# A four-layer transformer kernel: new head tiles copied before the output scale, the log forget gate turned onto 128 partitions, the convolution's norm one row step later

## The reference

```python
# differential attention, 8 heads; q, k: two maps of 64 each, v: 128
p = softmax(mask(q @ k.T * scale - slope_h * distance))      # per map
a = p[0] - lam * p[1]
o = rmsnorm(a @ v, g_sub) * (1 - lambda_init)

# odd mixer: forgetting attention (8 heads of 64) beside a conformer convolution
log_f = log_sigmoid(p[..., 1536:1544] + forget_b)            # (512, 8)
cum = cumsum(log_f, axis=positions)
logits[t, s] = q_t . k_s / 8 + cum[t] - cum[s]               # causal
y_c = softmax(logits) @ v
h = a * sigmoid(b)                                           # 512 channels
h = causal_dwconv(h, 31 taps) + dw_b
y_d = silu(layer_norm(h over channels) * cn_g + cn_b)
out = concat(y_c, y_d) @ w_out
```

## Time and profile before

| | us |
|---|---|
| median of 3 runs | 2386.34 (2384.98 to 2386.59) |
| the profiled execution | 2386.98 |
| its span | 2385.2 |
| PE busy in the span | 2304.6 (97%) |
| DVE, ACT, POOL busy | 722.7, 706.6, 1036.3 |
| granted TensorE clock, mean | 0.987 |

### The profile page before, as it was taken

How to read it: one execution, slowest core, us unless ns; L and a number is a source line. 1 busy time by engine, 2 the same in 40 slices (tenths; PEclk the granted TensorE clock), 3 DMA queues, 4 the chain that set the end, 5 groups by cost and what they waited for, 6 DMA issues and landing times.

```text
span 2385.2 us, 24593 instructions
## 1 busy us (share of the span) xinstructions
PE 2304.6 (97%) x10287; PEld 1847.2 (77%) x10287; DVE 722.7 (30%) x1361; ACT 706.6 (30%) x992; POOL 1036.3 (43%) x358
## 2 busy tenths in 40 slices
PE   8999999999999989999999999999998998999998
PEld 6667888887677768888878878888876666888887
DVE  6535000004566350000057310000169635000003
ACT  2453221222333232212222232222252563221221
POOL 3124554553333245545445555545432224554543
PEclk9999999999999999999999999999999999999999
DMA  4113323221211132322222323222320112323221
GB/s 166 72 71 124 106 89 106 88 85 69 112 54 54 53 106 88 106 89 97 97 92 92 105 106 100 94 97 88 102 75 29 56 58 80 132 88 106 89 88 53
DMA packets 32222, 212.60 MB, mean 89 GB/s; under 512 B 3568, under 2 KB 4720, under 8 KB 9072
## 3 DMA queue, kind: packets, MB, share of 16 engines
q1 hardware_dynamic: 32112, 211.03, 25.6%
HBM read 208.92 MB, written 2.10 MB: 88 GB/s over the span
## 4 chain that ended last, share of the span: by engine, by line
PE 89%; DVE 8%; ACT 2%; issue 1%; POOL 0%; DMA 0%; DVEq 0%; SPq 0%
PE bank L894 17%; PE bank L896 17%; PE bank L895 17%; PE bank L944 9%; PE bank L946 9%; PE bank L945 9%; PE bank L925 3%; DVE bank L1894 2%; PE bank L1004 2%; PE bank L930 1%; PE bank L1077 1%; PE bank L1324 1%; PE bank L982 1%; DVE X L1577 1%; PE bank L1245 1%
## 5 line engine op out<-in xcount | busy, mean ns | idle before, releaser
L754 POOL TENSOR_TENSOR wlo<-raw,whi 128x2048 fp32r<-128x2048 f32 (+4 forms) x183 | 842.1, 4604 | 664.4 <-ACT whi L432 664.4
L894 PE MATMUL bank<-XH,whi 128*128 128x512 f32 x1824 | 720.5, 395 | 9.6 <-POOL wlo L808 6.3
L896 PE MATMUL bank<-XH,wlo 128*128 128x512 f32 x1824 | 712.4, 391 | 0.0
L895 PE MATMUL bank<-XL,whi 128*128 128x512 f32 x1824 | 712.1, 390 | 0.0
L432 ACT CAST whi<-raw 128x2048 fp32r<-128x2048 f32 (+4 forms) x183 | 348.4, 1907 | 392.5 <-PE bank L944 304.5
L894 PEld LDWEIGHTS bank<-XH,whi 128*128 128x128 f32 x1824 | 343.9, 189 | 97.1 <-issue 18.6
L896 PEld LDWEIGHTS bank<-XH,wlo 128*128 128x128 f32 x1824 | 343.8, 188 | 72.8
L895 PEld LDWEIGHTS bank<-XL,whi 128*128 128x128 f32 x1824 | 344.2, 189 | 69.1
L1600 DVE TENSOR_TENSOR hf<-sil,bank 128x512 f32<-128x512 f32 x88 | 60.5, 688 | 902.9 <-PE bank L896 855.1
L768 POOL TENSOR_TENSOR HL<-hf,HH 128x512 fp32r<-128x512 f32 x88 | 114.0, 1295 | 400.2 <-ACT HH L470 400.2
L944 PE MATMUL bank<-whi,HH 128*128 128x512 f32 x704 | 274.4, 390 | 0.0
(11 more groups left out here) (258 smaller groups left out, 2120.9 us busy)
## 6 DMA issues: line engine op xcount, KB each, us to landing
raw<-w_ffn_gu SPq DMA_DIRECT2D x88, 1024.0 KB, 4.8
raw<-w_ffn_dn SPq DMA_DIRECT2D x40, 1024.0 KB, 4.8
raw<-w_diff_in SPq DMA_DIRECT2D x7, 1536.0 KB, 6.7
GB<-gb SPq DMA_DIRECT2D x8, 1024.0 KB, 6.9
raw<-w_ev_in SPq DMA_DIRECT2D x6, 1024.0 KB, 4.9
raw<-w_od_in SPq DMA_DIRECT2D x4, 1536.0 KB, 6.3
raw<-w_mla_pair SPq DMA_DIRECT2D x4, 1088.0 KB, 5.5
raw<-w_mla_o SPq DMA_DIRECT2D x4, 1024.0 KB, 5.9
```

The costliest lines, as they stand in the source:

```text
L754: pool.tensor_tensor(wlo[:, off:off + size], raw[:, off:off + size], whi[:, off:off + size].bitcast(F32), ALU.subtract).then_inc(lo_ready, 1)
L894: release(pe.matmul(out, whi[:, off:off + P], xh, start=start, stop=False))
L895: pe.matmul(out, whi[:, off:off + P], xl, start=False, stop=False)
L896: return pe.matmul(out, wlo[:, off:off + P], xh, start=False, stop=stop)
```

## The change

- Differential heads: in step j = 3 DVE copies the new k tile first and runs `scale_head` after it.
- The forget logits are written to `lfx` (8 by 512), four small matmuls on PE turn them into 32 columns of bank 3 on 128 partitions, the chain runs on tiles of 128 by 32, and four matmuls turn the result back to 8 by 512 in bank 3, from which the scan reads. The first four stand between the two tiles of the second gate pair, the last four between taps 7 and 8 of PE's convolution. ACT's Abs waits for the turned tile.
- DVE's taps: 24, 20, three times 6, and up to 6 in each row step, in place of 28, 28, three times 7, and up to 4.
- Rows, statistics, norm and columns of the convolution come one row step later; silu moves from step 11 to step 12, behind the weight split of that step.
- In the last pair `odd_out(0)` moves to the front of step 12, `odd_out(1)` to its end, and `odd_out(2)` to the end of step 15.

```diff
-        lfz, lfa, lfe, lfu, lfl, lfd, lfi, lfr = (sb(f"lf{n}", [8, S], F32, lf_stack) for n in "zaeuldir")
+        lfx, lf0 = (sb(f"lf{n}", [8, S], F32, lf_stack) for n in "x0")
+        lfz, lfa, lfe, lfu, lfl, lfd, lfi, lfr = (sb(f"lf{n}", [P, 8 * NB], F32, lf_stack) for n in "zaeuldir")
...
-            act.wait_ge(tile_free, tiles.at())
+            act.wait_ge(small_dve, 2)
             act.activation(lfa[:], lfz[:], ACT.Abs).then_inc(small_act, 1)
...
-                if s in (6, 7):
-                    keep_rows((1, 3)[s - 6])
-                if s in (9, 10):
-                    keep_cols((0, 2)[s - 9])
+                if s in (7, 8):
+                    keep_rows((1, 3)[s - 7])
+                if s in (10, 11):
+                    keep_cols((0, 2)[s - 10])
...
-                if s == 8:
+                if s == 9:
                     act.wait_ge(cn_ready, 1)
...
-                if s == 11:
+                if s == 12:
+                    split_w()
                     act.wait_ge(cols_kept, 4)
...
-                if qb == 1 and p < 3 or s in (12, 14):
+                if qb == 1 and p < 3 or s == 14:
                     split_w()
...
-            unit_into(GLU_BANKS[1])
+            forget = tiles.n
+            off = begin_unit()
+            tile(GLU_BANKS[1][0], [off + 2 * k * P for k in range(KD)])
+            pe.wait_ge(tile_free, forget)
+            claim(3)
+            for t in range(NB):
+                ins = pe.matmul(bank[3][:, 8 * t:8 * t + 8], lfx[:, t * P:(t + 1) * P], ident[0:8, 0:8], start=True, stop=True)
+            ins.then_inc(lt_done, 1)
+            tile(GLU_BANKS[1][1], [off + (2 * k + 1) * P for k in range(KD)])
...
-            conv_taps(range(0, 16))
+            conv_taps(range(0, 8))
+            pe.wait_ge(ls_ready, 1)
+            for t in range(NB):
+                ins = pe.matmul(bank[3][0:8, t * P:(t + 1) * P], lfz[:, 8 * t:8 * t + 8], ident, start=True, stop=True)
+            ins.then_inc(lt_done, 1)
+            conv_taps(range(8, 16))
...
-                elif qb:
-                    odd_out((1, 5, 7)[qb - 1])
+                elif qb != 1:
+                    odd_out((0, None, 5, 7)[qb])
...
-                if p == 3 and qb < 3:
-                    odd_out((0, 4, 6)[qb])
+                if p == 3:
+                    odd_out((1, 4, 6, 2)[qb])
...
-            odd_out(2)
             odd_attend(3)
...
-                    if j == 3:
-                        scale_head(h - 1)
                 for t in finished(DIFF_SLOTS[2 * j] + DIFF_SLOTS[2 * j + 1], (KD,) * 3) if h < 7 else ():
                     copy_tile((dVT, dQ[1 - h % 2], dK[1 - h % 2])[t][:], t)
+                if h and j == 3:
+                    scale_head(h - 1)
...
-            take(lambda: dve.tensor_scalar(lfz[:], bank[2][0:8, :], parm[0:8, PCOL["f_b"]:PCOL["f_b"] + 1], None, ALU.add))
+            take(lambda: dve.tensor_scalar(lfx[:], bank[2][0:8, :], parm[0:8, PCOL["f_b"]:PCOL["f_b"] + 1], None, ALU.add))
+            link(dve.memset(lf0[:], 0.0))
+            dve.wait_ge(lt_done, 1)
+            dve.tensor_copy(lfz[:], bank[3][:, 0:8 * NB]).then_inc(small_dve, 1)
...
+            dve.tensor_tensor(lfz[:], lfz[:], lfr[:], ALU.subtract).then_inc(ls_ready, 1)
+            dve.wait_ge(lt_done, 2)
+            dve.tensor_tensor_scan(cum[:], bank[3][0:8, :], lf0[:], 0.0, ALU.add, ALU.add).then_inc(cum_ready, 1)
 
             glu(1)
-            taps(28)
+            taps(24)
             glu(2)
-            taps(28)
+            taps(20)
             glu(3)
...
             for t in range(3):
-                taps(7)
+                taps(6)
...
-                taps(min(4, len(taps_left)))
-                if s == 6:
+                taps(min(6, len(taps_left)))
+                if s == 7:
                     row_stats(0)
-                if s == 7:
+                if s == 8:
                     row_stats(1)
                     row_stats(2)
-                if s == 8:
+                if s == 9:
                     row_stats(3)
```

More of the change, by code:

```diff
@@ L365, in build @@
         cum_ready = sem("cum_ready")
+        lt_done = sem("lt_done")
+        ls_ready = sem("ls_ready")
         mem_ready = sem("mem_ready")
@@ L642, in _ @@
             act.activation(lfe[:], lfa[:], ACT.Exp, scale=-1.0).then_inc(small_act, 1)
-            act.wait_ge(small_dve, 2)
+            act.wait_ge(small_dve, 3)
             act.activation(lfl[:], lfu[:], ACT.Ln).then_inc(small_act, 1)
@@ L708, in _ @@
                     odd_high(p - 1)
-                if s in (6, 7):
-                    keep_rows((1, 3)[s - 6])
-                if s in (9, 10):
-                    keep_cols((0, 2)[s - 9])
+                if s in (7, 8):
+                    keep_rows((1, 3)[s - 7])
+                if s in (10, 11):
+                    keep_cols((0, 2)[s - 10])
                 for m in range(2) if s else ():
                     keep_p(fPT[m], 6 + m, (s - 1) % 4)
-                if s == 5:
+                if s == 6:
                     keep_conv(3, conv_done, 3)
-                if s in (5, 6):
-                    keep_rows((0, 2)[s - 5])
-                if s == 8:
+                if s in (6, 7):
+                    keep_rows((0, 2)[s - 6])
+                if s == 9:
                     act.wait_ge(cn_ready, 1)
@@ L723, in _ @@
                                        scale=root[:, t:t + 1]).then_inc(rows_scaled, 1)
-                if s in (9, 10):
-                    keep_cols((1, 3)[s - 9])
-                if s == 11:
+                if s in (10, 11):
+                    keep_cols((1, 3)[s - 10])
+                if s == 12:
+                    split_w()
                     act.wait_ge(cols_kept, 4)
@@ L1465, in _ @@
                         head_steps(off, ODD_SLOTS[7])
-                elif qb:
-                    odd_out((1, 5, 7)[qb - 1])
[L1468 to L1471, removed]
+                elif qb != 1:
+                    odd_out((0, None, 5, 7)[qb])
+                if s in (7, 8):
+                    rows_of((1, 3)[s - 7])
+                if s in (10, 11):
+                    cols_of((0, 2)[s - 10])
                 for m in range(2) if s else ():
@@ L1477, in _ @@
                     off = begin_unit()
-                if p == 3 and qb < 3:
-                    odd_out((0, 4, 6)[qb])
[L1480 to L1483, removed]
+                if p == 3:
+                    odd_out((1, 4, 6, 2)[qb])
+                if s in (6, 7):
+                    rows_of((0, 2)[s - 6])
+                if s in (10, 11):
+                    cols_of((1, 3)[s - 10])
             los.add(4)
@@ L1906, in _ @@
             dve.tensor_scalar(lfu[:], lfe[:], 1.0, None, ALU.add).then_inc(small_dve, 1)
-            dve.wait_ge(small_dve, 2)
+            dve.wait_ge(small_dve, 3)
             link(dve.tensor_scalar(lfd[:], lfu[:], 1.0, None, ALU.subtract))
@@ L1919, in _ @@
             link(dve.tensor_scalar(lfz[:], lfz[:], 0.0, None, ALU.min))
-            link(dve.tensor_tensor(lfz[:], lfz[:], lfr[:], ALU.subtract))
-            link(dve.memset(lfd[:], 0.0))
-            dve.tensor_tensor_scan(cum[:], lfz[:], lfd[:], 0.0, ALU.add, ALU.add).then_inc(cum_ready, 1)
+            dve.tensor_tensor(lfz[:], lfz[:], lfr[:], ALU.subtract).then_inc(ls_ready, 1)
+            dve.wait_ge(lt_done, 2)
+            dve.tensor_tensor_scan(cum[:], bank[3][0:8, :], lf0[:], 0.0, ALU.add, ALU.add).then_inc(cum_ready, 1)
             glu(1)
-            taps(28)
+            taps(24)
             glu(2)
-            taps(28)
+            taps(20)
             glu(3)
```

## The result

| | before | after |
|---|---|---|
| median | 2385.88 us (2382.66 to 2387.38, 18 runs) | 2390.24 us (2386.50 to 2393.29, 18 runs) |
| ratio | | 1.0018 (95% interval 1.0012 to 1.0025) |
| the profiled execution, its span | 2386.98, 2385.2 | 2393.15, 2391.3 |
| granted clock, mean | 0.987 | 0.986 |

The changed kernel is slower by 4.4 us, 0.18%. I had forecast no change: 2386.0, in a range of 2377.5 to 2391.0. The time is inside the range, and 0.18% is still in the class "within 0.2%" to which I gave 0.58, but the interval leaves out no change: the edit did cost time.

What follows compares the result with a forecast made beforehand. PE, busy 97% of the span, was taken as the bound, DVE in the odd mixer's opening. Terms -6.5 - 5.7 + 5.3 + 3.7 + 2.9 = -0.3 us gave a median near 2386.0, range 2377.5 to 2391.

Steps and rivals of the forecast that it cites:

- heads: Differential heads 1 to 6: copying k before the scale removes a 1.18 us PE wait each, 0.1 paid back: -6.5 us.
- opening: Odd mixer's opening: PE's first logits start at 1845.4 against 1851.08, once DVE's copy of k is done: -5.7 us.
- logits 0 to 5: Row steps 0 to 5: DVE's extra taps and ACT's late first exponentials delay PE's logits: +5.3 us.
- logits 5 to 12: Steps 9 and 10: norm and weight split ahead of step 10's exponentials stall PE 2.1 us, plus 1.6 clock loss: +3.7.
- logits 12 to `odd_attend(3)`: Steps 12 to 15: losses of 8.7 us, including a stall of about 5.0 in step 13, against 5.8 before: +2.9.
- T: The time of PE's first logits in the odd mixer, from which steps 0 to 5 were counted.
- the stall in step 3: Odd mixer, row step 3: PE stalls about 3.7 us for banks 6 and 7, behind DVE's taps and gate bias.
- The clock after the step 10 wait: After PE's 2.1 us stall for bank 3 in step 10, the lower clock costs 1.6 us more.
- The lead: Rival, chance 0.27: norm and silu find room from step 6 on, last two terms vanish: 2379.4, or 2374.
- stay low for 12 us more: Rival, chance 0.11: PE runs at 1.2 GHz 12 us longer between steps 9 and 14, losing 6 us: 2392.
- Bank 7: Rival, chance 0.04: in the heads the scale slips 1 us behind the copy, so bank 7's late release cancels the gain: 2392.5.
- the three things that were to prove the prediction wrong: L1407's step 10 wait or the second L982 wait under 1 us, or step 4 logits over 4 us earlier, heads apart.

Runs made afterwards that it cites:

- the swap: Changed kernel with ACT's weight split for row step 0 ahead of its copy of convolution group 2: 2378.87 us, ratio 0.9974; same exchange in kernel before: 2385.45.
- the heads and a tap plan: Kernel before with the new heads order, ACT's weight split ahead of group 2's copy, taps 28, 22, three times 4, then 6 a row step: 2368.81 us, 0.9930.

## Why the prediction was wrong, point by point

The terms are read from the profiled executions (us, a plus is later than before). The two traces differ by 1.3 us at the logits of head 1 already, ahead of all of this. Each term is a difference of two distances within a trace, so this shift does not enter. In kernels without an edit in a stretch, the distance repeats to 0.2 us, but in that of the table's last row only to about 1 us (36.0 to 37.2).

| step of the prediction | forecast | traces | alone, by medians |
|---|---|---|---|
| heads | -6.5 | -6.4 | -6.3 |
| opening | -5.7 | +3.4 | |
| logits 0 to 5 | +5.3 | +4.5 | |
| logits 5 to 12 | +3.7 | +3.6 | +1.0 (rows) |
| logits 12 to `odd_attend(3)` | +2.9 | +1.5 | +0.9 |

**Heads.** Right, in size and mechanism. From the first logits of head 1 to those of head 7 it was 161.6 us and is 155.2, -6.4 in six heads. The six waits of v's transposes are 0.2 us, forecast 0.1.

**Opening: the step that failed.** The prediction put PE's logits on DVE's copy of k: "18 taps and three copies (14.2 + 1.9) at 1845.3. PE's logits start at 1845.4 against 1851.08: -5.7". The copy came on time. But in the next part it said itself that group 2 "now ends 0.7 us before PE's first logits" and that ACT's copy, the split and the table load follow it, and there I asked only what this does to the exponentials. The split is no work of ACT alone. Its high part is what POOL waits for, and POOL's low part is what PE's step 0 begins with. One line more would have given it: with T - 0.7 for the end of group 2, 0.6 for the copy and 2.75 for the split, POOL begins at T + 2.6 and PE's logits come at T + 9.3, not at T. Measured were 1849.00 against 1845.4 - 5.5, which is 9.1 later, and the swap gave 9.3 back. The rest of the opening was right: PE late by 4.5 us (forecast 4.3), the scan 4.5 later, DVE's copy on time. By the single edits, the tap plan gives -1.2 at the first logits and turning the gate +4.5, together the +3.4 of the table but for 0.1: here the parts add. The tap plan gains so little because of the missed wait for POOL: with the split moved ahead, the same taps are worth 10.5. With the missed term the sum is -0.3 + 9.1 = +8.8, the others unchanged; the runs gave +4.4.

**What else was off.** In the traces my four other terms were together 2.2 us too dear (+5.4 forecast, +3.2 read). In the first steps the stall in step 3 was 2.5 us, not 3.7, and the forecast's way to it was wrong in part: ACT did not hold the first exponentials, since the split that was to hold them now ended before the logits (ACT is idle for 6.66 us ahead of them). From the logits of step 0 to those of step 3 it was 18.8 us before and after; all of the +4.5 came in steps 3 and 4. After the wait of 5.4 us in step 13 the granted clock was 0.76 over 7 us, 1.7 us lost, where I had 2.9. The clock after the step 10 wait fell in the profiled execution of the changed kernel, as forecast (0.59 over 3.8 us, 1.6 us lost), but not after 1.94 us in the kernel with the rows alone, and not after 1.96 us in the one with the swap. I had charged it as certain. Another 0.4 us lies outside the terms (+0.9 ahead of the opening, -1.3 behind the mixer), and 1.8 is the profiled pair (6.2) against the medians (4.4): 8.8 - 2.2 - 0.4 - 1.8 = 4.4. What makes executions of the changed kernel differ was not tried.

**Steps 9 to 15.** The waits came as worked out, 1.9 for 2.1 and 5.4 for 5.0. Alone, neither of the two moves can be told from no change, and the forecasts (+3.7 and +2.9) lie above and at the upper ends of the two intervals (3.3 and 2.9). By medians the parts alone (heads, gate, taps, rows, last pair) add up to -6.3 + 3.4 + 1.9 + 1.0 + 0.9 = +0.9 us, and the changed kernel is at +4.4. Each of the five is known to about 2 us, so by whole runs it stays open whether they cost more together than apart.

**The rivals.** The lead was not kept, and the clock did not stay low for 12 us more. A late weight split was none of the rivals. Bank 7 did not replace the copy. The rule on table switches in the Trainium skill, "ScalarE: Activation LUTs", section "What ACT_TABLE_LOAD costs", a drain of about 1.38 us at each switch, does not show after the change either: ACT's timeline in step 12.

```profile
1952.35 1.93 ACT L435 CAST whi<-raw 128x2048 fp32r<-128x2048 f32 x1
1954.29 1.28 ACT L733 ACT_TABLE_LOAD   x1
1955.59 2.93 ACT L733 ACTIVATE fC<-fC,parm 128x512 f32<-128x512 f32 x4
```

The load starts 0.01 us after the split ends, and silu 0.02 after the load. The wait that holds these switches is 5.4 us, where the rule, with two switches in it, would have made it about 8.2 (an estimate: the drain that the Trainium skill gives, taken twice).

**The range.** None of the three things that were to prove the prediction wrong came (waits under 1 us in step 10 or 13, step 4's logits over 4 us early); none of them looked at the opening, where its sign (a wait of 2.5 us for DVE's copy) failed. 2377.5 to 2391.0 held the time, but for no reason of its own: its upper end was made of a clock that stays low and of bank 7, neither of which came, and the missed 9.1 us were halved by terms that were too dear.

## What to carry to other kernels

When a stall goes, list everything that the waiting engine waits for at that point, with the time at which each is ready, and not only the one that the profile names: the 8.29 us wait had a second condition 3.7 us behind the first. Follow each instruction that is made later to the end of its chain, across engines: a high part made late on ACT is a low part made late on POOL and a matmul made late on PE. And when, in the code order of one engine, an instruction with ready inputs stands behind one with late inputs, this costs nothing until that chain is the last to be ready; the swap of two lines was worth nothing in the kernel before and 10.6 us in the changed one, and with the heads and a tap plan it gives 2368.81, 17 us under the kernel before. Before comparing starts in two traces, find an event ahead of the edit and count from it: here the starts alone gave 2.6 and 3.1 us for turning the gate, where every pair has 4.5.

## What the runs showed of the hardware

Waits of nearly equal length at the same place were followed by either level of TensorE's clock: after 1.95 us the lower one (1.2 GHz, matmuls of 0.63 us; the stretch of 3.8 us below has a granted clock of 0.59), after 1.94 and 1.96 us the full one (2.4 GHz, 0.39 us, granted clock 1.00 over the same length). The loss after the wait of 11.2 us is no larger than after the one of 8.29 (granted clock 0.56 over 7 us after each). Stretches of the changed kernel (length, PE busy, other engines, granted clock), to be read beside the earlier trace rows:

```profile
1849.00:1856.00 7.00, 7.00 (x23) 5.62 (x24) 5.46 (x12) 1.58 (x6) 0.00 (x0) 0.56 0.61 225
1937.30:1941.10 3.80, 3.80 (x12) 2.70 (x10) 1.93 (x9) 2.33 (x6) 0.00 (x0) 0.59 0.76 269
1964.30:1971.30 7.00, 6.87 (x24) 5.02 (x25) 1.21 (x7) 1.93 (x5) 2.52 (x2) 0.76 0.01 2
```

The same stretch as the second one, in the kernel with the rows alone and in the changed kernel with the swap:

```profile
1932.40:1936.20 3.80, 3.80 (x15) 2.27 (x13) 2.31 (x10) 2.42 (x6) 0.00 (x0) 1.00 0.80 252
1925.20:1929.00 3.80, 3.80 (x13) 2.12 (x13) 2.40 (x10) 2.56 (x6) 0.00 (x0) 1.00 0.83 263
```

On DVE an operation on 128 by 32 took 0.18 to 0.20 us, where the same one on 8 by 512 took 0.41 to 0.68 (one 3.50, beside POOL's low part), and the reciprocal 0.35 for 3.34: both have 4096 elements, so in these operations the width along the row sets the time and not the number of elements. Four small float32 products on PE took 1.05 us with 8 columns each and 1.04 with 128. And runs of the changed kernel spread over 6.8 us, those of the kernel before over 4.7.
